# Weight conversion ahead of the evacuations in the second feed-forward, and the last differential query spread over three attention units

## The reference

```python
def diff_attend(q, k_all, v_all, lam):
    ...
        s = jnp.einsum('bhqcd,bhkcd->bhcqk', qb, k_all).astype(jnp.float32) * (DIFF_DH ** -0.5)
        p = jax.nn.softmax(s, axis=-1)
        a = (p[:, :, 0] - lam.astype(jnp.float32) * p[:, :, 1]).astype(v_all.dtype)
        return jnp.einsum('bhqk,bhkd->bhqd', a, v_all)
```

```python
def conv_ffn(h, w_up, conv_w, conv_b, w_down):
    z = h @ w_up
    zc = conv_w[2] * z + conv_w[1] * shift_right(z, 1) + conv_w[0] * shift_right(z, 2) + conv_b
    g, u = zc[..., :D_FF], zc[..., D_FF:]
    return (jax.nn.gelu(g, approximate=True) * u) @ w_down
```

## Time and profile before

| | |
|---|---|
| median of three runs | 1706.14 us |
| lowest and highest | 1703.86, 1706.66 us |
| the profiled execution's own time | 1712.11 us |
| its span | 1710.5 us |
| TensorE busy, mean granted clock | 1595.0 us (93%), 0.968 |
| DVE, ACT, POOL busy | 935.5, 730.8, 124.4 us |

### The profile page before, as it was taken

One profiled execution on the slowest core, in us unless ns is written; L12 is line 12 of the kernel. 1 busy time (PEld: TensorE's weight loads), 2 busy tenths in 40 slices (PEclk: granted clock), 3 DMA queues, 4 the chain that ended last, 5 costly groups with the idle time before them and its releaser, 6 DMA issues.

```text
span 1710.5 us, 19159 instructions
## 1 busy us (share of the span) xinstructions
PE 1595.0 (93%) x7606; PEld 1249.4 (73%) x7606; DVE 935.5 (55%) x1441; ACT 730.8 (43%) x1132; POOL 124.4 (7%) x89
## 2 busy tenths in 40 slices
PE   8998999789899999999998999999779898999989
PEld 1776876577688888888786777887657676887765
DVE  4665787785744433335637454547455664266643
ACT  4453445565332222233525566456363333233332
POOL 0100213530000000000100111200100000000000
PEclk9999999699999999999999999999889998999999
DMA  9441111102333233223222121333031222322221
GB/s 365 165 156 38 50 59 53 50 1 107 135 128 136 76 112 108 99 68 109 83 98 69 56 72 53 121 95 105 19 99 62 66 83 71 112 87 86 71 85 54
DMA packets 47950, 156.60 MB, mean 92 GB/s; under 512 B 5587, under 2 KB 10323, under 8 KB 47350
## 3 DMA queue, kind: packets, MB, share of 16 engines
q1 hardware_dynamic: 47280, 152.00, 26.5%
q10 hardware_dynamic: 582, 3.38, 0.5%
HBM read 153.26 MB, written 2.10 MB: 91 GB/s over the span
## 4 chain that ended last, share of the span: by engine, by line
PE 65%; DVE 20%; ACT 11%; issue 3%; POOL 1%; DMA 0%; ACTq 0%; DVEq 0%; POOLq 0%
PE pall L2097 14%; PE pall L2099 14%; PE pall L2098 14%; DVE wlo L1242 4%; ACT whi L564 3%; DVE tmp L1953 2%; ACT tmp L1186 2%; DVE tmp L1950 2%; DVE pall L1899 2%; PE pall L2581 2%; PE pall L2133 1%; PE pall L2115 1%; PE pall L2117 1%; PE pall L2116 1%; PE pall L2135 1%
## 5 line engine op out<-in xcount | busy, mean ns | idle before, releaser
L1242 DVE TENSOR_TENSOR wlo<-raw,whi 128x1024 fp32r<-128x1024 f32 (+2 forms) x261 | 290.6, 1115 | 386.0 <-ACT whi L564 386.0
L564 ACT ACTIVATE whi<-raw 128x1024 fp32r<-128x1024 f32 (+2 forms) x263 | 246.5, 939 | 152.3 <-PE pall L2099 116.4
L2097 PE MATMUL pall<-h5h,whi 128*128 128x512 f32 x320 | 127.3, 398 | 19.4 <-DVE wlo L1242 19.4
L2099 PE MATMUL pall<-h5h,wlo 128*128 128x512 f32 x320 | 125.6, 393 | 0.0
L2098 PE MATMUL pall<-h5l,whi 128*128 128x512 f32 x320 | 125.5, 392 | 0.0
L2097 PE MATMUL pall<-h2h,whi 128*128 128x512 f32 x320 | 124.5, 389 | 0.0
L2098 PE MATMUL pall<-h2l,whi 128*128 128x512 f32 x320 | 124.5, 389 | 0.0
L2099 PE MATMUL pall<-h2h,wlo 128*128 128x512 f32 x320 | 124.5, 389 | 0.0
L2097 PEld LDWEIGHTS pall<-h5h,whi 128*128 128x128 f32 x320 | 60.7, 190 | 37.0 <-issue 24.7
L2097 PE MATMUL pall<-ch,whi 128*128 128x512 f32 x176 | 71.1, 404 | 14.2 <-DVE cl L1980 14.2
L1186 ACT ACTIVATE tmp<-pall,vec 128x512 f32<-128x512 f32 x44 | 34.0, 778 | 103.8 <-DVE pall L1899 103.8
(11 more groups left out here) (460 smaller groups left out, 3657.1 us busy)
## 6 DMA issues: line engine op xcount, KB each, us to landing
raw<-in_weights SPq DMA_DIRECT2D x204, 512.0 KB, 3.4
mraw<-in_wmod SPq DMA_DIRECT2D x32, 512.0 KB, 5.0
mod<-in_weights SPq DMA_DIRECT2D x16, 512.0 KB, 12.3
raw<-in_weights SPq DMA_DIRECT2D x25, 256.0 KB, 2.6
raw<-in_weights SPq DMA_DIRECT2D x32, 192.0 KB, 2.3
xT<-in_x SPq DMA_DIRECT2D x1, 2048.0 KB, 17.0
xT<-in_x ACTq DMA_DIRECT2D x1, 2048.0 KB, 8.3
out_y<-xT SPq DMA_DIRECT2D x8, 256.0 KB, 2.1
```

The costliest lines, as they stand in the source:

```text
L564: e.activation(whi[j % 3][:, 0:cols(j)], raw[j % 4][:, 0:cols(j)], ACT.Copy).then_inc(s.hi, 1)
L1242: e.tensor_tensor(wlo[j % 3][:, 0:n], raw[j % 4][:, 0:n], f(whi[j % 3][:, 0:n]), ALU.subtract).then_inc(s.lo_v, 1)
L2097: e.matmul(o_, a[:, kk, :], xh(k), start=(k == 0), stop=False)
L2099: mm = e.matmul(o_, b[:, kk, :], xh(k), start=False, stop=(k == nk - 1))
```

## The change

Three edits of order; no operation is added or taken away, and no transfer is moved in its queue.

1. On ACT, first step of dv: `turned_keys(0)` stands ahead of `decays(2)`.
2. Differential attention: ACT's `query_root(3)` moves from unit 0 to unit 2. DVE's `query_norm(3)` at unit 0 is cut into three steps: `newton` at unit 2, the scaled query at unit 3, `turn_halves` at unit 4. POOL's `rotated` of this query moves from ahead of `gated(2)` to unit 4, behind that unit's scaling and ahead of its low part of the mix.
3. Second feed-forward on ACT: each `hi` stands ahead of the `conv` that it followed.

```diff
             for n in range(4):
                 hi(J[("dv", 2 * n)] + 2)
+                if n == 0:
+                    turned_keys(0)
                 for i in GAPS_AT[n]:
                     decays(i)
                 if n == 1:
                     first_scores(0)
-                turned_keys(n)
+                if n:
+                    turned_keys(n)
...
-                if n == 0:
+                if n == 2:
                     query_root(3)
...
                     if jj >= 2:
                         used(("f2g", jj, 0))
+                        hi(J[("f2g", jj, 0)] + 3)
                     conv(2 * jj, ffn_bank("f2w", ("f2g", "f2u"), 0, jj), jj)
                     if jj >= 2:
-                        hi(J[("f2g", jj, 0)] + 3)
                         used(("f2u", jj, 0))
+                        hi(J[("f2u", jj, 0)] + 3)
                     conv(2 * jj + 1, ffn_bank("f2w", ("f2g", "f2u"), 1, jj), 22 + jj)
-                    if jj >= 2:
-                        hi(J[("f2u", jj, 0)] + 3)
                     gelu(jj)
...
+            def last_query(step):
+                if step == 0:
+                    newton("dq3", bank(DQS[3]), 512, 64)
+                elif step == 1:
+                    query_scaled(3)
+                else:
+                    turn_halves(4 + 3)
...
-                if n == 0:
-                    query_norm(3)
+                if n in (2, 3, 4):
+                    last_query(n - 2)
...
-            for i in range(4):
+            for i in range(3):
                 rotated(4 + i, Qd[:, i, :])
...
                 e.tensor_scalar(e1, e1, sd[:, col + 3:col + 4], nlam, ALU.mult, ALU.mult).then_inc(s.dnl, 1)
+                if n == 4:
+                    rotated(4 + 3, Qd[:, 3, :])
```

More of the change, by code:

```diff
@@ L1519, in out_norm, with query_scaled @@
                 e.scalar_tensor_tensor(HN[h], bank(4 + h % 2), v("gla_norm_g"), r, ALU.mult, ALU.mult).then_inc(s.hov, 1)
-            def query_norm(i):
-                newton(f"dq{i}", bank(DQS[i]), 512, 64)
+            def query_scaled(i):
                 r = inv(f"dq{i}")
@@ L1525, in query_norm @@
                 e.scalar_tensor_tensor(tmp[2][:, :], bank(DQ[i]), v("diff_q_norm_g"), r, ALU.mult, ALU.mult).then_inc(s.hnt, 1)
+            def query_norm(i):
+                newton(f"dq{i}", bank(DQS[i]), 512, 64)
+                query_scaled(i)
                 turn_halves(4 + i)
+            def last_query(step):
[5 more added lines that the diff above has]
+                    turn_halves(4 + 3)
             for i in range(4):
```

## The result

The changed kernel takes 1655.37 us in the median of four runs (1654.45 to 1656.52); the kernel before, beside it, 1706.39 us (four runs, 1703.86 to 1706.66). The ratio is 0.9705, interval 0.9688 to 0.9721: 3.0% faster, 51.0 us. The forecast was 1655.4 us. The profiled execution took 1654.45 us, with a span of 1652.8.

The account below looks back on a forecast made before the run. TensorE, busy 93% of the span, was taken as the bound, so gains come from its idle time or clock. Edits 3, 1 and 2 save 41.1 + 4.6 + 5.0 = 50.7 us: 1706.1 to 1655.4 us, range 1645 to 1668.

Parts of the forecast that it names:

- The working's chain of 8.5 us for DVE alone: Second feed-forward: DVE's own work per hidden tile after edit 3 takes 8.5 us, below TensorE's 10.9.
- DVE was to wait for TensorE and not for line 564: Second feed-forward, profile after: DVE's idle time in each tile is a wait for TensorE, not for line 564.
- the 0.6 us of the prediction: Down stages: the last `cl` is ready with 0.6 us to spare, twice, so the 7.10 us waits go.
- One wait was to be left, of 2.4 us: Start of the second feed-forward: TensorE still idles 2.4 us from 1329.6 for a low part.
- I take 2.7: Second feed-forward: 2.7 us lost to TensorE's lower clock behind the remaining wait, bounds 0 and 2.7.
- a wait of about 1.6 us: dv, edit 1: the 4.18 us wait goes and one of about 1.6 us stands before the transposes.
- with transposes and scores I take 2.9 us: Attention, edit 2: 2.9 us charged for TensorE at the lower clock, with its value product, transposes and scores.
- The charge for contention with POOL, 1.0 us: Attention units four and five: POOL's rotation slows DVE's combination by 0.7 us, with the keys' low part 1.0 in sum.
- The rival in which contention takes the whole gain: Attention: POOL and DVE contend more at the new place, so edit 2 gives nothing; 1660.4 us, chance 0.05.
- the chain didn't stay the bound: Rival, second feed-forward: conv behind `hi` delays the taps, 14 us of the 41 are lost; 1669 to 1672, chance 0.09.
- the loads were never late: Rival "Slower", second feed-forward: `hi` ahead of conv makes the evacuation wait for a load; 1716 us, chance 0.01.
- the front stages didn't give back what they gained: Rival, dv and attention: the front stages give their stalls back and only edit 3 counts; 1665 us, chance 0.08.

Follow-up runs that it names:

- The deeper version: The changed kernel with the second to sixth tiles of the second feed-forward asking for weight pieces 5 or 4 ahead, not 3; 1650.94 us, ratio 0.9676.

## Why the prediction was right

**Edit 3: 41.1 us expected, 41.3 measured alone, 41.5 by the timelines.** The mechanism held. DVE stood idle for a high part that ACT made too late in its program; the run with DVE's taps first shows that this idle time, and not ACT's order by itself, was the cost. The working's chain of 8.5 us for DVE alone is 8.54 in the tiles where it catches up. One sign was put too strongly: DVE was to wait for TensorE and not for line 564, and 0.39 us per tile of that wait are left, which cost TensorE nothing. Both waits on `cl` are gone, and their return with only one call moved (2.5 us for two) says that the margin there is small, as the 0.6 us of the prediction said. One wait was to be left, of 2.4 us: it is 2.48.

One term was mis-sized: "I take 2.7", for the lower clock behind that wait. Windows around it:

```profile
1316.00:1318.00 2.00, 2.00 (x5) 1.54 (x6) 1.77 (x3) 0.05 (x1) 0.00 (x0) 0.50 0.63 145
1318.00:1320.00 2.00, 2.00 (x8) 1.56 (x7) 1.39 (x3) 1.53 (x2) 0.00 (x0) 0.67 0.29 117
1320.00:1322.00 2.00, 2.00 (x10) 1.69 (x9) 1.97 (x3) 1.73 (x2) 0.00 (x0) 1.00 0.01 4
```

The clock did fall to the lower level of 1.2 GHz. The lost time is 2 x 0.50 in the first window, 2 x 0.33 in the second and nothing in the third: 1.7 us, not 2.7. The row of before from which I took the cost had 4.43 us of idle time ahead of it, and the clock stayed down longer there. The deeper version, which has neither the wait nor the lower clock, gains 4.4 us in these stages: 2.5 for the wait, and 1.9 left for the clock.

**Edit 1: 4.6 us expected, 3.6 measured alone (1.2 to 4.6 by its interval).** The transposes were forecast at 142.3, behind a wait of about 1.6 us; they came at 142.35, behind 1.73. (The copies of the first scores, written at 141.1, would by the terms given start at 141.4; they started at 141.19.) That is 4.6 us by the profile of before. The run with this edit alone places them at 143.16, only 3.8 us sooner, but it was 0.87 us late before it came to the edit; counted from the first transposes it saves 4.6 as well. The term was right, and 4.6 is just within the interval of the measured time.

**Edit 2: 5.0 us expected, 8.1 measured alone (4.8 to 9.4), 5.7 by the timelines.** The steps that the prediction worked out for DVE hold: unit 1 starts 3.3 us after unit 0 (forecast 3.4), DVE waits for the root at unit 2 for 1.74 us (1.7), POOL isn't waited for in unit 1. Both of its charges were mis-sized, in opposite directions.

The charge for TensorE, "with transposes and scores I take 2.9 us", was too large. DVE waited for TensorE's scores twice, 0.47 and 1.06 us in the rows above, 1.5 together. The clock did stay at the lower level almost to unit 5, as these windows of the changed kernel show, for TensorE alone:

```profile
320.00:322.00 2.00, 2.00 (x11) 0.50 0.00 0
322.00:324.00 2.00, 2.00 (x13) 0.85 0.00 0
```

In the profile of before the window from 330 to 332 is at 0.50 too, and that from 332 to 334 at 0.81, again some 2 us ahead of unit 5. So the lower clock was there, and cost DVE less than was taken: of the 2.9 us only 1.4 came from a row, and the rest was taken for transposes and scores without one. DVE's path of 25.3 us (forecast 25.4) and 1.5 make 26.8, a gain of 6.5 over the 33.3 of before in units 0 to 5.

The charge for contention with POOL, 1.0 us, was too small and in the wrong place. What was slowed were other instructions, here with POOL's beside them:

```profile
295.24 1.26 POOL L2038 TENSOR_TENSOR rS<-AT,rS 128x512 f32<-128x512 f32 x1
295.63 1.42 DVE L1257 SCALAR_TENSOR_TENSOR R<-W,R 128x512 f32<-128x512 f32 x1
...
311.78 1.26 POOL L2064 TENSOR_TENSOR mixl<-rS,mixh 128x512 fp32r<-128x512 f32 x1 [1.58 <-ACT mixh L849]
311.93 1.66 DVE L1257 SCALAR_TENSOR_TENSOR R<-W,R 128x512 f32<-128x512 f32 x1
...
322.84 0.69 DVE L1481 TENSOR_TENSOR tmp<-tmp,sint 128x512 f32<-128x512 f32 x1
322.89 1.80 POOL L2024 TENSOR_TENSOR tmp<-tmp,cost 128x512 f32<-128x512 f32 x1
```

Line 1257 takes 0.69 us elsewhere (line 1255 of the kernel before, at 300.22). It lost 0.7 us ahead of unit 0 and 1.0 at unit 2. The keys' low part of unit 1 lost 0.6 (1.51 for 0.94), the combination of unit 5 0.2 (1.21 for 1.02): 2.5 us in sum. The 0.7 ahead of unit 0 is what the gain of 6.3 us up to unit 8 has to be reduced by. The rival in which contention takes the whole gain is refuted.

The Trainium skill (GPSIMD Engine Reference, Key points) says that vector instructions with two SBUF inputs contend with GpSimd. That agrees with these rows, but the estimate that I had worked out by it, 0.72 us for each of three instructions in units four and five, doesn't: the sine product and the low part there took their usual 0.69 and 0.94, and the combination lost 0.2.

**The sum.** 50.7 us expected, 51.0 measured (47.6 to 53.2 by the interval). By the timelines the parts are 4.6, 5.7 and 41.5, 51.8 in sum, where 4.6, 5.0 and 41.1 were expected. So the parts were right within 1 us, with three terms in them that were not: the clock in edit 3 (2.7 for 1.7), TensorE's charge in edit 2 (2.9 for 1.5), and contention (1.0 for 2.5), which partly cancel. That forecast and median agree within 0.03 us is luck; the interval alone is far wider. The choice to take the saving from the median and not from the profiled execution was worth 6 us, and the run of edit 3 alone justifies it: most of the extra time was in the clock of an untouched stage.

The rivals: the chain didn't stay the bound (no tile waits but one), the loads were never late, and the front stages didn't give back what they gained, apart from the 0.7 us ahead of unit 0.

## What to carry to other kernels

Where two engines hand one chain to and fro, work of theirs that doesn't belong to the chain (here the weights' parts) should stand where its engine would wait for the other. Here a new order on either engine brought nearly all of it. Once the chain is shorter than the bound engine's time per tile, only starts and ends of stages are left. A wait at such a start wasn't mended by pulling one item forward, which handed the wait to the next one: the depth had to be raised over several tiles, until the backlog was worked off. And compare a saving worked out from a profile with the medians: the same code took some 5 us more or less from one profile to the next.

## What the hardware showed unexpectedly

A wait of TensorE costs more than its length when the clock is lower behind it. In this feed-forward, behind waits of 2.48, 2.49, 3.35, 4.43, 4.44 and 4.95 us on a low part and of 7.10 us on `cl` it was granted the lower level for 3 us or more. Behind one of 1.84 us on `cl`, in the run with the gate's call alone, the windows stay at 1.00, and so they do around the waits of 0.9 to 1.6 us, one per tile, in the kernel before (1352 to 1422 us):

```profile
1404.00:1406.00 2.00, 1.34 (x6) 1.12 (x7) 1.08 (x2) 0.63 (x2) 0.00 (x0) 1.00 0.00 0
1406.00:1408.00 2.00, 2.00 (x11) 1.63 (x10) 0.75 (x1) 1.21 (x2) 0.00 (x0) 1.00 0.38 98
```

And identical code can run a stretch of 20 us at 0.83 in one execution and at 1.00 in another (940 to 960 us, above). That alone is worth 3.4 us, nearly as much as edit 1.

Where DVE and POOL slowed each other, it was in these rows the one that began second: DVE at 295.63 and 311.93, each 0.4 us or less behind POOL's start, took 1.42 and 1.66 us for 0.69; at 322.84 DVE began 0.05 us ahead of POOL and took its 0.69, and POOL's product took 1.80 us, for 1.26 of its instructions of this size in the rows above. So the price of contention depended on which engine came first, and not only on which instructions overlapped.
